# Placement of matmul operands in SBUF, and one VectorE step moved behind GpSimd, in a decoder layer

## The reference, cut to what matters

```python
x = x + 0.5 * swiglu_ffn(x, ffn1...)          # first feed-forward, f = 0
h = rms_norm(x); ... = split(h @ w_in)        # gated DeltaNet, MoBA and memory attention
x = x + concat(y_gdn, y_moba, y_mem) @ w_out
x = x + 0.5 * swiglu_ffn(x, ffn2...)          # second feed-forward, f = 1
def swiglu_ffn(x, gain, w_gate, w_up, w_down):
    h = rms_norm(x, gain)
    return (silu(h @ w_gate) * (h @ w_up)) @ w_down
```

## Time and profile before

| what | value |
|---|---|
| median of 3 runs | 984.42 us (984.19 to 984.7) |
| the profiled execution's own time | 984.34 us |
| its span, first to last instruction | 982.5 us |
| TensorE busy | 977.0 us (99%) |
| VectorE, ScalarE, GpSimd busy | 689.4, 443.8, 513.4 us |
| granted TensorE clock | 1.00 |

### The profile page before, as it was taken

The page is one execution under the profiler, slowest core; times in us unless marked ns, Lnnn a source line. Parts: engine busy times, 40 slices in busy tenths (PEclk is TensorE's granted clock), DMA queues, the critical chain, the costliest instruction groups (busy, mean ns, idle before and its releaser), DMA issues.

```text
span 982.5 us, 16493 instructions
## 1 busy us (share of the span) xinstructions
PE 977.0 (99%) x6818; PEld 862.3 (88%) x6818; DVE 689.4 (70%) x1093; ACT 443.8 (45%) x654; POOL 513.4 (52%) x297
## 2 busy tenths in 40 slices
PE   9999999999999999999999999999999999999998
PEld 7888999999999988788877888888999999999997
DVE  6894976676666487863548764789987776667746
ACT  7742444344443472434356764534444344443441
POOL 0355865676656433543252301644976676756741
PEclk9999999999999999999999999999999999999999
DMA  8432322332223312321221001323132332223312
GB/s 312 158 129 82 117 91 94 129 129 85 80 95 129 119 54 86 127 88 44 86 72 60 2 3 43 115 77 109 44 117 99 129 130 95 78 86 129 130 43 86
DMA packets 15914, 95.32 MB, mean 97 GB/s; under 512 B 2016, under 2 KB 2400, under 8 KB 5600
## 3 DMA queue, kind: packets, MB, share of 16 engines
q1 hardware_dynamic: 15696, 94.23, 26.8%
q10 hardware_dynamic: 144, 0.05, 0.0%
HBM read 92.17 MB, written 2.10 MB: 96 GB/s over the span
## 4 chain that ended last, share of the span: by engine, by line
PE 94%; POOL 2%; DVE 2%; issue 1%; ACT 1%; DMA 0%; SPq 0%; DVEq 0%
PE bank L2028 51%; PE bank L2154 32%; POOL wlo L538 2%; PE bank L2185 1%; PE bank L2467 1%; PE bank L2553 1%; PE bank L2471 1%; PE bank L2493 1%; PE bank L2581 1%; PE bank L2570 1%; PE bank L2515 1%; PE bank L2537 0%; POOL wlo L521 0%; DVE t_ffn_sum L1348 0%; DMA x<-x_in 0%
## 5 line engine op out<-in xcount | busy, mean ns | idle before, releaser
L2154 PE MATMUL bank<-t_ffn_hi,whi 128*128 128x256 f32 x952 | 266.0, 279 | 1.0 <-POOL wlo L538 1.0
L2154 PE MATMUL bank<-t_ffn_lo,whi 128*128 128x256 f32 x952 | 265.4, 279 | 0.0
L2154 PE MATMUL bank<-t_ffn_hi,wlo 128*128 128x256 f32 x952 | 265.4, 279 | 0.0
L538 POOL TENSOR_TENSOR wlo<-sums,whi 128x512 fp32r<-128x512 f32 x136 | 185.1, 1382 | 125.0 <-ACT whi L745 124.9
L521 POOL TENSOR_TENSOR wlo<-raw,whi 128x1024 fp32r<-128x1024 f32 (+1 forms) x36 | 124.6, 3475 | 166.3 <-ACT whi L618 150.4
L538 POOL TENSOR_TENSOR wlo<-raw,whi 128x512 fp32r<-128x512 f32 x102 | 171.8, 1698 | 37.4 <-ACT whi L745 37.3
L2154 PEld LDWEIGHTS bank<-t_ffn_hi,whi 128*128 128x128 f32 x952 | 178.8, 188 | 1.8 <-POOL wlo L538 1.2
L2154 PEld LDWEIGHTS bank<-t_ffn_hi,wlo 128*128 128x128 f32 x952 | 179.0, 188 | 0.0
L2154 PEld LDWEIGHTS bank<-t_ffn_lo,whi 128*128 128x128 f32 x952 | 178.3, 187 | 0.7
L2028 PE MATMUL bank<-ahi,whi 128*128 128x512 f32 x388 | 153.2, 395 | 0.4 <-POOL wlo L521 0.4
L2028 PE MATMUL bank<-ahi,wlo 128*128 128x512 f32 x388 | 151.2, 390 | 0.0
(11 more groups left out here) (342 smaller groups left out, 1415.4 us busy)
## 6 DMA issues: line engine op xcount, KB each, us to landing
raw<-fast_in SPq DMA_DIRECT2D x34, 1024.0 KB, 4.9
raw<-stream SPq DMA_DIRECT2D x26, 1024.0 KB, 4.9
raw_down<-fast_in SPq DMA_DIRECT2D x19, 1024.0 KB, 7.0
raw<-stream SPq DMA_DIRECT2D x7, 512.0 KB, 8.1
out<-x SPq DMA_DIRECT2D x7, 256.0 KB, 2.0
x<-x_in SPq DMA_DIRECT2D x3, 512.0 KB, 8.8
memx<-mem_in SPq DMA_DIRECT2D x2, 512.0 KB, 11.3
raw_gate<-stream SPq DMA_DIRECT2D x1, 1024.0 KB, 4.8
```

The costliest lines, as they stand in the source:

```text
L538: nc.gpsimd.tensor_tensor(in_ring(wlo, ring_at, n), whole[:, PIECE * at:PIECE * (at + 1)], in_ring(whi, ring_at, n).bitcast(F32), ALU.subt ...
L2154: ins = E.matmul(psum[bank][:, HALF * h:HALF * (h + 1)], a, b[:, k, :], start=start and k == 0 and m == 0, stop=k == K2 - 1 and m == 2, sk ...
```

## The change

1. `hlo` begins 64 bytes later (64 modulo 256 in place of 0). Two asserts are loosened by as much. `mksq`, `p6` and `u2`, which follow `hlo`, move along.
2. In the first feed-forward T_2 and T_B21 exchange their places; both stay at 64 modulo 256.
3. In the second feed-forward T_2 goes to `kt_at + 8192 - 192`, which is 64 modulo 256, and T_B21 to `kt_at - 288`, which is 224 modulo 256 as before.
4. In body 0 of the second feed-forward VectorE waits ahead of `down_low` until GpSimd has made 13 pieces of that body (q = 0 to 12).

```diff
-        hlo, _, nxt2 = place("hlo", [P, 4, T], F32R, at=nxt)
+        hlo, _, nxt2 = place("hlo", [P, 4, T], F32R, at=nxt + PAD)
...
-        assert nxt2 <= z_at
+        assert nxt2 <= z_at + PAD
...
-        z_t, cq_t, a_hi_t, a_lo_t, kt_t = z_at + PAD, cq_at + PAD, a_hi0 + PAD, a_lo0 + PAD, kt_at - 32
-        t_at = [[z_t, z_t + EIGHT, z_t + 2 * EIGHT, a_hi_t, a_hi_t + EIGHT, a_lo_t, a_lo_t + EIGHT],
-                [a_lo_t, a_lo_t + EIGHT, cq_t, kt_t, kt_t + EIGHT, z_t, z_t + EIGHT]]
+        z_t, cq_t, a_hi_t, a_lo_t = z_at + PAD, cq_at + PAD, a_hi0 + PAD, a_lo0 + PAD
+        t_at = [[z_t, z_t + EIGHT, z_t + 2 * EIGHT, a_hi_t + EIGHT, a_hi0 + PAD, a_lo_t, a_lo_t + EIGHT],
+                [a_lo_t, a_lo_t + EIGHT, cq_t, kt_at + EIGHT - 3 * PAD, kt_at - 288, z_t, z_t + EIGHT]]
...
                     if i == 0:
                         combine(f, 0, 1)
+                        if f == 1:
+                            dve.wait_ge(f_lo, POOLED * F0 * f + 13)
                         down_low(f, 0)
```

## The result

The changed kernel takes 987.78 us (median of 7, 987.57 to 988.26) against 984.42; the ratio is 1.0035, 95% interval 1.0025 to 1.0045. It is slower by some 3.4 us where 3.5 us faster was forecast (980.9). Lines in the changed kernel are two further down: L2030 is the L2028 of before, L2156 the L2154.

What follows compares the result with a forecast made beforehand. TensorE is always busy with almost no waits, so the pace at which matmuls follow one another bounds the kernel. From 984.34 us, -1.76 - 0.89 - 0.78 = -3.43 gave 980.9 us, range 979.0 to 982.4.

Steps and rivals of the forecast that it cites:

- The reading of the pace: Sevenths: a tile at 64 keeps the pace it finds, 1.36 or 1.413 us; one at 224 turns it.
- T_2's new place: Second feed-forward, T_2 from 224 to 64: it no longer turns the pace, -1.76 us in sum.
- The step that failed: Down products, `hlo` from 0 to 64: each matmul reading `hlo` wins 2.2 ns, -0.78 us; zero not excluded.
- The upper bound: Down products with `hlo` at 64: all 1,062 matmuls run at the entry pace, 4.6 ns slower each, +4.9 us.
- the down product does not settle: Rival: changing offsets keep the down product at entry pace, +4.9 us less 2.65 of the other parts, 986.6; chance 0.18.
- part of it: Rival: T_2 at 64 may still turn the pace, or `hlo` cost 1 to 2 ns a matmul: 982.5 to 984.3; chance 0.09.
- The wait: Body 0, second feed-forward: q = 13 goes before the down split; -1.22 us, 0.33 back through a late add, -0.89.
- stay covered: Pieces for body 1 come 1.4 us later but are used over 7 us into the down product, costing nothing.
- Offsets do nothing: Rival: the pace is not the tiles' doing, only the wait's gain is left: 983.45 us; chance 0.06.
- The swap in the first feed-forward: T_2 and T_B21 change places, both at 64: costs nothing, as the pace there depends on neither.

Runs made afterwards that it cites:

- e5: The kernel before with T_2 and T_B21 placed as in the change, `hlo` at 0 and no wait: 982.32 us, ratio 0.9981.
- e6: e2 with T_B21 of the second feed-forward at 64 too, so no tile at 224: 986.0 us, ratio 1.0015 to the kernel before.
- e7: e2 with T_B21 at 224 in the first feed-forward as well, T_4 taking its place: 980.79 us, ratio 0.9949 to the kernel before.
- e2: The changed kernel with `hlo` back at offset 0: 982.34 us, ratio 0.9980 to the kernel before.
- e1: The kernel before with `hlo` alone 64 bytes later: 989.25 us, ratio 1.0048.
- e3: The kernel before with `hhi` and `hlo` both at 64: 986.41 us, ratio 1.0023.
- e4: The kernel before with the wait ahead of the down split alone: 984.24 us against 984.2, ratio 0.9998.
- e8: The kernel before with the wait and, in body 1 of the second feed-forward, output tile 3's add ahead of the weight sums: 984.82 us, ratio 1.0003.
- e9: e7 without the wait: 979.27 us against 984.37 for the kernel before, ratio 0.9954.
- e10: The kernel before with `hlo` alone 32 bytes later: 990.88 us, ratio 1.0063.

## Why the prediction was wrong, step by step

**The reading of the pace was right in the main.** A tile at 64 keeps the pace it finds, one at 224 turns it (e5, e6, e7). T_2's new place was put at -1.76 us and is worth that where the down product is left as before: -1.76 in e2's profile, and 982.32 against 984.12 us in e5. Two things are missing from the rule. The first T_B21 behind a down product does not turn the pace in the kernel before: T_4, T_B22 and the next T_B21 take (783.42 - 779.17) / 3 = 1.417 us, and only that second T_B21 brings 1.36. And a gap turned it as well (e6, body 0).

**The step that failed is `hlo`**, taken at -0.78 us "from the row of the commonest pace at 64, which is the nearest row there is". It cost +4.9 (e1). The nearest row was one of 256-column matmuls with both parts at 64; e3 shows that even with both parts at 64 a 512-column stream loses 2.1 ns a matmul. The rest of the loss comes with two parts at different offsets: 231.9 ns with 0 and 64. The upper bound, 1,062 matmuls at the entry pace, was +4.9 us and is what happened: the rival "the down product does not settle", with a chance of 0.18. That a settled stream could itself be slow, as with both at 64 or with 0 and 32, was in no rival beyond the 1 to 2 ns of "part of it"; that the entry pace (231.4) and the lasting one (231.9) nearly agree is not explained, and the exact hit may be luck. The argument against this rival, that sevenths at 224 don't settle and cost little, compared tiles whose two parts are alike.

**A second effect was not foreseen:** the down product as it now runs also changes what the T_B21 behind it does. In even bodies of the changed kernel the fast pace now comes after the first T_B21 and the second turns it back, so the next body begins slow. T_B21, T_4 and the second T_B21 of body 2 begin at:

```profile
780.19 0.28 PE L2156 MATMUL bank<-t_ffn_hi,whi 128*128 128x256 f32 x1
...
781.61 0.28 PE L2156 MATMUL bank<-t_ffn_hi,whi 128*128 128x256 f32 x1
...
784.33 0.28 PE L2156 MATMUL bank<-t_ffn_hi,whi 128*128 128x256 f32 x1
```

T_4 and T_B22 take (784.33 - 781.61) / 2 = 1.36 us, where the kernel before has the slow pace. Of T_2's -1.76 only some -0.5 is left (sevenths -1.76 less the gap's -1.22). That is most of why the time is 987.8 and not the rival's 986.6.

**The wait was read rightly from one execution and priced too high.** q = 13 went first and the gap of 1.22 us closed, as forecast; body 0's down product lost 0.01 (changed kernel) or 0.13 us (e2) where 0.33 was put, and 0.3 (changed kernel) to 0.68 us (e2) were lost one body later, which the sentence that the pieces "stay covered" missed: it looked at the pieces and not at the transfer that waits for them. So the -0.89 came out near -0.8 in the changed kernel's profile and -0.34 in e2's. The other error was to take one profile's order for all: in the second order there is nothing to gain (e4). In the medians the wait shows no gain over 0.1 us in any of four comparisons (e4 and e8 with before, e2 with e5, e7 with e9), each uncertain by some 1 us either way (by the ratios e7 is 0.5 us ahead of e9). How often either port order occurs was not measured beyond the twelve profiled executions, six of each.

**The other rivals.** "Offsets do nothing" falls with e1, e6 and e7. The Trainium skill's rule that TensorE waits on no one (SBUF — State Buffer, Who interferes with whom) was set against 1.36 and 1.413 us for one tile. The rule is on engines that wait for each other, which no run here tests for TensorE; what falls is what the prediction drew from it: e6 adds 3.7 us by one tile's offset, so placement does set TensorE's pace here, by whatever way. The trace agrees with its rule on a VectorE instruction with two SBUF inputs and GpSimd's reads, with 2.37 against 1.23 us for the same instruction. The swap in the first feed-forward cost nothing, as put: 19.79 us a body in the changed kernel.

**Open.** What inside TensorE or its reads makes the two paces and the slow streams is not shown; the runs show only that offsets and what ran before decide it. Not tried were `hhi` at 64 with `hlo` at 0, equal offsets other than 0 and 64, and `hlo` moved without `mksq`, `p6` and `u2`.

## What to carry to other kernels

Where TensorE is always busy, read the start-to-start time of equal matmuls, tile by tile: it shows losses that no busy share and no wait shows. Where the high and the low part of an operand alternate, try them first at the same offset modulo 256 (of the four pairs tried here both at 0 was the fastest at 512 columns), and move one tile at a time, since a tile's offset can change the pace of those after it. Before an edit is priced by a port order or a gap, look in a second profile for whether the order holds.

## What the runs showed of the hardware that was not expected

- 512-column matmuls whose two moving operands alternate between offsets 0 and 64 did not settle in a round of three and averaged some 232 ns against 226.8 (e1, the changed kernel); with 0 and 32 they did, at 233.3 in the first feed-forward, 11.20 us for 48 against 10.92 (e10); with both at 64 also, at 228.9, in one body at 233.4 (e3).
- The pace of 256-column matmuls, 113.3 or 117.8 ns at one granted clock, is handed from tile to tile; 12 matmuls on one tile at 224 turned it (in the kernel before not straight behind a down product), and a wait of 0.64 us did too (e6); one such tile was worth 3.7 us in nine bodies (e6 against e2) and, in the sevenths of its profile, 3.3 us in eight (e7).
- Two engines that started within 0.02 us of each other got the way in either order, in six of twelve profiles each: GpSimd where it started 8 to 18 ns ahead of VectorE, VectorE where it was 1 to 3 ns behind. In eleven of the twelve the order still told 30 us later.
